# Expert feed-forward: wider weight slices in fewer slots, picks with the table as the stationary operand, prompt rows moved as 128 pieces

## What is computed

```python
aff = softmax(xf @ w_router)                  # (t, 16)
cap = 2 * t // 16                             # 16 of 128 rows, 128 of 1024 rows
gate, idx = top_k(aff.T, cap)
xe = xf[idx]                                  # (16, cap, 1024)
h = silu(xe @ w_e1) * (xe @ w_e3)             # three matrices of 1024x1024 per expert
ye = (h @ w_e2) * gate[..., None]
out = zeros_like(xf).at[idx].add(ye)
```

## Time and profile before

| | |
|---|---|
| median of 3 executions | 4532.65 us (4531.85 to 4542.73) |
| the profiled execution: first to last instruction | 4535.4 us; the page gives no other time for it |
| PE busy, share of the span | 3940.0 us, 87% |
| DVE / ACT / POOL busy | 2176.8 (48%) / 970.4 (21%) / 1048.6 (23%) us |
| DMA moved | 836.27 MB, mean 184 GB/s |
| mean granted TensorE clock | 0.924 |
| `experts`, first layer / second layer | about 1352 to 2260 us / 3580 to 4491 us |

### The profile page before, as it was taken

The page is one execution under the profiler, slowest core; times in us unless marked ns, Lnnn a source line. Parts: engine busy times, 40 slices in busy tenths (PEclk is TensorE's granted clock), DMA queues, the critical chain, the costliest instruction groups (busy, mean ns, idle before and its releaser), DMA issues. The chain is left out here.

```text
span 4535.4 us, 81543 instructions
## 1 busy us (share of the span) xinstructions
PE 3940.0 (87%) x34010; PEld 3088.9 (68%) x34010; DVE 2176.8 (48%) x4932; ACT 970.4 (21%) x1898; POOL 1048.6 (23%) x1092
## 2 busy tenths in 40 slices
PE   4999967888777999999779997788869599999994
PEld 3444546676347999999744444566654399999994
DVE  3335046566555445444453341566646544454444
ACT  2233134444110000000033322443431100000001
POOL 0036034453210000011040440445512001000003
PEclk9999978888888999999989998888879799999997
DMA  7556353331528999999664653243233299999995
GB/s 266 173 192 229 127 125 77 77 71 36 192 72 243 276 276 270 280 278 269 183 233 150 241 192 89 71 95 78 66 110 129 105 278 270 274 278 276 271 279 179
DMA packets 822587, 836.27 MB, mean 184 GB/s; under 512 B 92008, under 2 KB 667560, under 8 KB 816076
## 3 DMA queue, kind: packets, MB, share of 16 engines
q1 hardware_dynamic: 740172, 711.10, 52.5%
q10 hardware_dynamic: 70432, 81.03, 5.3%
q0 software_dynamic: 11616, 38.94, 3.8%
HBM read 698.83 MB, written 132.10 MB: 183 GB/s over the span
## 5 line engine op out<-in xcount | busy, mean ns | idle before, releaser
L2525 PE MATMUL ffn_hb<-ffn_xT,ffn_w 128*128 128x144 f32 x8192 | 1055.4, 288 | 11.2 <-DVE ffn_xT L2638 6.5
L2525 PEld LDWEIGHTS ffn_hb<-ffn_xT,ffn_w 128*128 128x128 f32 x8192 | 1025.8, 191 | 14.1 <-DVE ffn_xT L2638 6.7
L521 PE MATMUL front_acc<-front_w,front_xmT 128*128 128x512 f32 (+2 forms) x2304 | 879.2, 541 | 17.7 <-DVE front_xmT L782 17.5
L521 PEld LDWEIGHTS front_acc<-front_w,front_xmT 128*128 128x128 f32 x2304 | 438.2, 192 | 444.7 <-issue 417.7
L2533 PE MATMUL ffn_acc<-ffn_hT,ffn_w 128*128 128x144 f32 x4096 | 550.2, 288 | 0.0
L2533 PEld LDWEIGHTS ffn_acc<-ffn_hT,ffn_w 128*128 128x128 f32 x4096 | 521.4, 191 | 0.8
L2573 ACT ACTIVATE ffn_en<-ffn_hb 128x144 f32<-128x144 f32 x256 | 74.6, 291 | 1483.0 <-PE ffn_hb L2525 1483.0
L2457 POOL DMA_INDIRECT ffn_xe<-scratch_xhat,ffn_g_idx x34 | 34.5, 1015 | 1376.2 <-DVEq L2627 1376.2
L2672 DVE TENSOR_TENSOR ffn_hT<-ffn_en,ffn_hb 128x144 f32<-128x144 f32 x256 | 77.7, 304 | 528.8 <-ACT ffn_en L2573 527.9
L2247 PE MATMUL mixer_acc<-mixer_wout,mixer_oT 128*128 128x512 f32 x576 | 256.6, 604 | 3.2 <-DMA mixer_wout<-in_w_out 1.7
L2596 DVE TENSOR_SCALAR_CACHE_REDUCE ffn_junk<-ffn_row,ffn_pair 128x128 f32<-128x128 f32 (+2 forms) x324 | 245.4, 757 | 6.3 <-DVE ffn_yp L2645 4.9
(11 more groups left out here) (324 smaller groups left out, 5206.0 us busy)
## 6 DMA issues: line engine op xcount, KB each, us to landing
ffn_w<-in_w_e SPq DMA_DIRECT2D x768, 512.0 KB, 6.4
x_res<-in_w_mod SPq DMA_DIRECT2D x40, 1024.0 KB, 5.6
x_res<-scratch_proj SPq DMA_DIRECT2D x36, 768.0 KB, 6.2
scratch_proj<-front_out ACTq DMA_DIRECT2D x90, 256.0 KB, 2.2
ffn_row<-scratch_affT SPq DMA_DIRECT2D x36, 576.0 KB, 6.3
front_w<-in_w_in ACTq DMA_DIRECT2D x8, 2048.0 KB, 12.3
scan_qk<-scratch_qkv SPq DMA_DIRECT2D x16, 1024.0 KB, 9.8
scratch_qkv<-x_res SPq DMA_DIRECT2D x18, 768.0 KB, 3.5
```

The lines of the kernel that those rows point to most:

```text
L521: mm = pe.matmul(acc[:, U % 2, 0:size], xmT[:, k, t * P:(t + 1) * P], w[:, n % 2, k, 0:size], start=k == 0, stop=k == KD - 1)
L2525: mm = pe.matmul(hb[:, b, i * CAP:(i + 1) * CAP], w[:, r, k, :], xT[:, s, k, :], start=k == 0, stop=k == KD - 1)
```

## The change

Weights come as four slices of 256 hidden columns (1 MB from each matrix) in three slots. The picks use the table `pair`, widened to 32 columns, as the stationary operand and `sel` as the moving one: sample tiles 1 to 8 go in turn to the four 32-partition strips of one PSUM block, so that two tiles add up in each strip; DVE copies the block to SBUF (`copy_picks`), PE transposes it (`turn_picks`), and DVE adds the four strips (`rank_picked`). The prompt's 16 rows of 1024 are gathered and scattered as 128 pieces of 128 columns, eight per row, so that one 128x128 transpose replaces the eight small ones, and `turn_y` is no longer split. The copies of `acc` write sample and prompt columns to two tiles. The diff, cut to its core:

```diff
-    RING = 4
-    PER = KF // RING
+    RING = 3
+    WIDTH = 2
+    PER = KF // WIDTH
...
-        w1, w3, w2 = (st.sb(x, [P, RING, KD, P]) for x in ("w1", "w3", "w2"))
-        xe, xp = st.sb("xe", [P, D]), st.sb("xp", [CAP_P, D])
+        w1, w3 = (st.sb(x, [P, RING, KD, WIDTH * P]) for x in ("w1", "w3"))
+        w2 = st.sb("w2", [P, RING, WIDTH, D])
+        xe, xp = st.sb("xe", [P, D]), st.sb("xp", [P, P])
...
-        yT = st.sb("yT", [P, KD, CAP])
+        yT, yTp = st.sb("yT", [P, KD, CAP_S]), st.sb("yTp", [P, KD, CAP_P])
-        pair = st.sb("pair", [P, TILES, 2])
+        pair = st.sb("pair", [P, TILES, 32])
+        found = st.sb("found", [P, 2 * P])
...
-                    for j in range(KF):
-                        r = j % RING
-                        sp.wait_ge(w_used[r], e * PER + j // RING + 1)
+                    for j in range(0, KF, WIDTH):
+                        r = slot_of(e, j)
+                        c = slice(j * P, (j + WIDTH) * P)
+                        sp.wait_ge(w_used[r], fills(e, j) + 1)
+                        sp.dma_start(w1[:, r], T["w_e1"][l, e, :, c].rearrange("(k p) n -> p k n", p=P)).then_inc(w_in[r], 16)
+                        sp.dma_start(w3[:, r], T["w_e3"][l, e, :, c].rearrange("(k p) n -> p k n", p=P)).then_inc(w_in[r], 16)
+                        sp.dma_start(w2[:, r], T["w_e2"][l, e, c, :].rearrange("(a p) n -> p a n", p=P)).then_inc(w_in[r], 16)
-                        if j == 1:
+                        if j == 0:
                             sp.wait_ge(ranked, e + 3)
...
-                    for src, n, k in ((ye, P, 0), (yp, CAP_P, 1)):
+                    for src, dst, k in ((ye, T["moe"], 0), (yp, pieces("moe"), 1)):
...
-                    for k in range(KD):
-                        mm = pe.transpose(trp[:, k * CAP_P:(k + 1) * CAP_P], xp[:, k * P:(k + 1) * P], B.ident[0:CAP_P, 0:CAP_P])
-                    mm.then_inc(turned, 1)
+                    pe.transpose(xpT, xp[:], B.ident).then_inc(turned, 1)
+                def turn_y(e):
+                    pe.wait_ge(yT_done, e * 2 + 3)
+                    for k in range(KD):
+                        pe.transpose(tr[:, k * P:(k + 1) * P], yT[:, k, :], B.ident)
+                    pe.transpose(ypT, yTp[:].rearrange("p k n -> p (k n)"), B.ident).then_inc(y_turned, 1)
+                def sum_picks(e):
                     pe.wait_ge(sel_done, e + 2)
                     for t in range(1, TILES):
-                        pe.matmul(slot_s, sel[:, t, :], pair[:, t, :], start=t == 1, stop=t == TILES - 1)
-                    pe.matmul(slot_p, sel[:, 0, 0:CAP_P], pair[:, 0, :], start=True, stop=True).then_inc(picked, 1)
+                        q = (t - 1) % 4
+                        pe.matmul(trp[32 * q:32 * q + 32, 2 * P:3 * P], pair[:, t, :], sel[:, t, :], start=t <= 4, stop=t > 4)
+                    pe.matmul(found_p, pair[:, 0, :], sel[:, 0, 0:CAP_P].unsqueeze(1).to_broadcast([P, KD, CAP_P]), start=True, stop=True).then_inc(summed, 1)
+                def turn_picks(e):
+                    pe.wait_ge(copied, e + 2)
+                    pe.transpose(slot_s, found[:, 0:P], B.ident)
+                    pe.transpose(slot_p, found[0:32, P:2 * P], B.ident[0:32, 0:32]).then_inc(picked, 1)
...
                     def up_products(j):
-                        pe.wait_ge(w_in[r], (e * PER + j // RING) * 48 + 49)
+                        if j % WIDTH == 0:
+                            pe.wait_ge(w_in[r], fills(e, j) * 48 + 49)
...
                     def down_products(j):
-                        mm.then_inc(w_used[r], 1)
+                        if j % WIDTH == WIDTH - 1:
+                            mm.then_inc(w_used[r], 1)
...
                     up_products(0)
                     if not first:
-                        turn_y(e - 1, 0)
+                        turn_y(e - 1)
                     up_products(1)
                     if first:
-                        pick(1)
+                        sum_picks(1)
                     down_products(0)
-                    if not first:
-                        turn_y(e - 1, 1)
+                    if first:
+                        turn_picks(1)
...
-                    pick(e + 2)
+                    sum_picks(e + 2)
                     down_products(KF - 1)
+                    turn_picks(e + 2)
...
+                        act.activation(yT[:, k, :], y[:, :, 0:CAP_S], ACT.Copy)
+                        ins = act.activation(yTp[:, k, :], y[:, :, CAP_S:], ACT.Copy)
...
+                def copy_picks(e):
+                    dve.wait_ge(summed, e + 2)
+                    dve.tensor_copy(found[:, 0:P], found_s).then_inc(own, step())
+                    dve.tensor_copy(found[0:32, P:2 * P], found_p).then_inc(own, step())
+                    dve.wait_ge(own, step.n)
+                    dve.sem_inc(copied, 1)
...
+                    dve.tensor_scalar(ye[:], tr[:], picks[:, e, 1:2], None, ALU.mult).then_inc(own, step())
+                    dve.tensor_scalar(yp[:], ypT, picks[:, e, 3:4], None, ALU.mult).then_inc(own, step())
...
+                    copy_picks(e + 2)
+                    dve.wait_ge(w_used[slot_of(e, KF - 1)], fills(e, KF - 1) + 2)
+                    k, y = by_piece(0)
+                    dve.tensor_copy(yT[:, k, :], y[:, :, 0:CAP_S]).then_inc(own, step())
+                    dve.tensor_copy(yTp[:, k, :], y[:, :, CAP_S:]).then_inc(own, step())
                     rank_picked(e + 2)
```

More of the change, by code:

```diff
@@ L2421, in experts, with by_piece, slot_of, fills @@
         part = lambda c: acc[:, c // PER_BANK, (c % PER_BANK) * CAP:(c % PER_BANK + 1) * CAP]
+        pieces = lambda name: T[name].rearrange("r (k c) -> (r k) c", c=P)
+        def by_piece(b):
+            n = min(PER_BANK, KD - b * PER_BANK)
+            return slice(b * PER_BANK, b * PER_BANK + n), acc[:, b, 0:n * CAP].rearrange("p (k c) -> p k c", c=CAP)
+        def slot_of(e, j):
+            return (e * PER + j // WIDTH) % RING
+        def fills(e, j):
+            return (e * PER + j // WIDTH) // RING
         def turns(eng, body):
@@ L2454, in gather @@
                 def gather():
[L2455 to L2457 removed]
+                    for dst, src, k in ((xe, T["xhat"], 0), (xp, pieces("xhat"), 1)):
+                        at = bass.IndirectOffsetOnAxis(ap=g_idx[:, k:k + 1].bitcast(U32), axis=0)
+                        pool.indirect_dma_start(dst[:], None, src, at).then_inc(gathered, 16)
                 def scatter(e):
@@ L2584, in _ @@
                 dve.memset(counts[:], 0.0).then_inc(own, step())
+                dve.memset(pair[:], 0.0).then_inc(own, step())
                 dve.tensor_tensor(later[:], B.masks[:, 1, :], B.ident, ALU.subtract).then_inc(own, step())
+                dve.wait_ge(own, step.n)
                 dve.tensor_copy(pair[:, :, 0], B.ids[:, 0:TILES]).then_inc(own, step())
@@ L2622, in index @@
                         dve.wait_ge(own, step.n)
-                    dve.tensor_copy(idx[:, 0:1], token[:, 0, bass.ds(e, 1)]).then_inc(own, step())
-                    dve.tensor_copy(idx[0:CAP_P, 1:2], token[0:CAP_P, 1, bass.ds(e, 1)]).then_inc(own, step())
+                    dve.tensor_copy(idx[:], picks[:, e, 0:4:2]).then_inc(own, step())
                     dve.wait_ge(own, step.n)
@@ L2681, in body @@
                                 index(s_idx, e - 1, None)
-                                output(e - 1, 0)
+                                output(e - 1)
                             dve.wait_ge(row_in, e * 16 + 49)
-                        if j == 1 and not first:
-                            output(e - 1, 1)
                         if j == 5:
@@ L2691, in body @@
                             rank_tile(t)
+                    copy_picks(e + 2)
[3 more added lines that the diff above has]
+                    dve.tensor_copy(yTp[:, k, :], y[:, :, CAP_S:]).then_inc(own, step())
                     rank_picked(e + 2)
-                    dve.wait_ge(w_used[RING - 1], e * PER + PER + 1)
-                    dve.tensor_copy(yT[:, 0:PER_BANK, :].rearrange("p k n -> p (k n)"), acc[:, 0, 0:PER_BANK * CAP]).then_inc(own, step())
                     dve.wait_ge(own, step.n)
```

84 lines of the change are left out of this document (35 added, 49 removed).

## The result

Four executions of the changed kernel took 4473.70 to 4477.68 us, median 4476.71; four of the kernel before, beside it, had a median of 4532.25. The ratio is 0.9878, with a 95% interval of 0.9866 to 0.9890. The forecast was 4473 in a range of 4455 to 4505, so time and sign came out as predicted. By the medians the gain is 55.5 us for the 59.8 forecast. The profiled execution after, the fastest of its four, took 4473.70 us and spans 4471.9; the span before was 4535.4.

A forecast was written before the change was run, and what follows sets the result against it. The prediction took TensorE to bound the expert stage. Net gains of 29.9 us per layer, 59.8 for two, brought the profiled 4535.4 us to 4475.6, or 4473 in terms of the median, in a range of 4455 to 4505.

The forecast's parts named there:

- TensorE bounds the stage, and what leaves its order is gained: Expert stage: PE is busy throughout at clock 1.00; each expert gains 2.09 us, for a period of 50.39 us.
- Turning x and y: Transposes in each expert: one 128x128 transpose replaces eight small ones; gain 0.48 us at `x`, 0.77 at `y`.
- The pick: Pick in each expert: four strips run at once, so it takes 1.06 us for 1.90, gain 0.84.
- The work put at nothing: `turn_picks`, `turn_y` and POOL's 128 pieces in mid stage: waits are covered by other work and cost nothing.
- Weights in mid stage: Weight loads in mid stage: 350 GB/s and no stall, with 286 GB/s as the bound if wider runs bring nothing.
- rival 2: Mid stage: DMA becomes the bound and PE waits for weights, up to 1 us per expert; 4475 to 4508; chance 0.07.
- Start of each layer: First expert: up 2 must wait for all of pair 1, costing 4.0 us per layer; first pick 0, 2 either way.
- End of each layer: Last `turn_y` and scatter: one undivided chain, DVE ends earlier, larger scatter gives back 0.3; gain 1.2 us per layer.
- The sum: Per layer: experts 1 to 15 gain 31.4, expert 0 1.3, end 1.2, start -4.0; net 29.9 us.
- 1: Rival on the pick: strips of 32 columns do not overlap, 1.3 us more per expert, 4520 us; chance 0.08.
- 3: Rival on the clock: it falls in each expert, costing 3.7 us in 31 experts, 4588 us; chance 0.06 with similar losses.
- 4: Rival on the weight loads: the wider slices are the gain; expected to lose some 8 us alone; no chance of its own.

The follow-up runs named there:

- the run with old picks: Changed kernel with the picks as before (two moving columns over 128 stationary ones, no transposes of picks): median 4491.32 us, ratio 0.9903.
- the run without cover: Changed kernel with `turn_picks` directly behind `sum_picks`, no down product between: median 4488.89 us, ratio 0.9916.
- the narrow run: Changed kernel with its slices set back to 128 columns in four slots of one: median 4467.41 us, ratio 0.9850.
- the run with one strip: Changed kernel with the sixteen pick passes written to one strip of 32 partitions instead of four: median 4513.63 us, ratio 0.9963.
- the two lighter kernels: Changed kernel with seven of eight `w3` products left out, all loads kept: 4298.58 us with 128-column slices in four slots, 4264.89 with 256-column slices in three.

## Why the prediction was right

*TensorE bounds the stage, and what leaves its order is gained.* Right: 2.02 us per expert (2.09 predicted), PE busy throughout, clock 1.00.

*Turning x and y.* `y`: 0.98 us, as predicted to the hundredth. `x`: 0.98 for the 1.08 predicted, gain 0.58 for 0.48; the 0.97 for the eight large transposes held the step to the small shape (0.87 without it), which the ninth, of their own shape, does not need.

*The pick.* The mechanism, four strips at once, was right, and the passes took 0.47 us for 0.44 predicted. The terms around them were mis-sized: entering costs 0.09 us, as put down, but the prompt's product takes 0.31 for 0.22, and the two transposes with their entry 0.48 (0.38 and 0.10) for 0.30. In all 0.47 + 0.09 + 0.31 + 0.48 = 1.35 us for 1.06, and the gain is 0.55 in place of 0.84; the run with old picks says 0.56. Most of the missing 0.29 is made good, by luck, by 0.10 at `x` and about 0.1 at seams that no step had counted: 0.55 + 0.58 + 0.77 + 0.1 = 2.0.

*The work put at nothing.* Right for `turn_picks` (0.63 us under 1.96, by the run without cover), for `turn_y` in mid stage and for POOL: none shows up as a wait in the windows.

*Weights in mid stage.* No wait, as predicted, but the reasoning failed in one step: "just enough and no more" at 275 / 0.96 = 286 GB/s. The old slices gave 315, and the narrow run, at just this bound, shows no wait in mid stage: the price that rival 2 hung on it had no ground. Nor was the 419 GB/s set against it a figure for the new slices: it belongs to runs of 4 KB and longer, and 1 KB runs gave 379 where they were waited for.

*Start of each layer.* The step that failed in size, hidden by an opposite error. From the row load to up 2 it was 1411.55 - 1401.96 = 9.59 us and is 15.12: 5.53 more; up 2 itself, at the lower clock, takes 6.48 for 5.86: 0.62 more, 6.15 in all for the 4.0 put down. The kernel with narrow slices, all else as changed, needs 1403.51 - 1393.80 = 9.71 us from the row load to up 2, so the slices make 5.41 of the 15.12; by the stage sums they cost 5.3 us per layer there and 6.0 alone. The 5.35 that the prediction had first, at 294 GB/s, was nearer than the 4.0 to which it came down for faster runs. The extra 1.57 MB at the 346 to 396 GB/s of the windows above would be 4.0 to 4.5 us by itself. That the rest is the gather of expert 1, which now falls wholly into the wait (issued at 1402.87 us; before at 1407.16, 4.4 us ahead of up 2), is argued, not shown. Against that, the stretch from the first pick to the row load shrank from 1401.96 - 1376.28 = 25.68 to 1396.49 - 1372.85 = 23.64: 2.04 us. Of these, 1.29 lie between the first pick and the turning of `x` (10.11 us before, 8.82 after), which "shorter products and added copies and transposes about cancel" had put at 0 with 2 to either side; the other 0.75, turning `x` of expert 0 at the low clock, had no term. From the first pick to the end of up 2 the sum is 41.13 before and 45.24 after, 4.1 more. The 4.0 was right as a sum by luck, and wrong in both its parts.

*End of each layer.* From ACT's first copy to the next stage's first load: 4491.35 - 4469.98 = 21.37 before, 4428.18 - 4408.24 = 19.94 after: 1.43 in the second layer for the 1.2 predicted, 2.00 in the first. POOL starts 4.78 us after ACT, where it was 6.80. The transposes start only 0.20 us later behind ACT's copy (1.09 for 0.89), not 0.6; the scatter and what follows it give back 0.59, not 0.3.

*The sum.* In the first layer it can be split without remainder, at the row loads, the turning of `x` in experts 0 and 15 and ACT's first copy of the last `acc`. Before (PE's and ACT's timelines):

```profile
2223.93 1.04 PE L2490 MATMUL ffn_tr<-masks_sb,ffn_xe 128*128 128x128 f32 x8
2241.52 0.83 ACT L2577 ACTIVATE ffn_yT<-ffn_acc 128x432 f32<-128x432 f32 x2 [5.64 <-PE ffn_acc L2533]
```

After:

```profile
2194.43 1.04 PE L2508 MATMUL ffn_tr<-masks_sb,ffn_xe 128*128 128x128 f32 x8
2210.30 0.49 ACT L2596 ACTIVATE ffn_yT<-ffn_acc 128x384 f32<-128x384 f32 x1 [4.60 <-PE ffn_acc L2553]
```

| stretch of the first layer | before | after | gain |
|---|---|---|---|
| row loads to turning `x` in expert 0 (1436.84, 1437.53) | 85.25 | 89.23 | -3.98 |
| fifteen experts, to turning `x` in expert 15 | 787.09 | 756.90 | 30.19 |
| to ACT's first copy (turning `x`, the pick's products) | 17.59 | 15.87 | 1.72 |
| to the next stage's first load | 23.68 | 21.68 | 2.00 |
| sum | 913.61 | 883.68 | 29.93 |

The prediction had -4.0, 31.4 for the fifteen experts, 1.3 and 1.2. That 29.93 meets its 29.9 so closely is luck: 1.2 too much in the experts stands against 0.4 and 0.8 too little behind them.

*The rivals.* 1: refuted as a description of the changed kernel, confirmed as a price by the run with one strip. 2: no wait in mid stage at either width. 3: the clock was 1.00 in mid stage, and in the first expert, where the old pick had the low clock behind it (down 0 took 3.90 us), down 0 behind the new pick takes 2.23; with the old picks in the changed kernel it took 3.40. 4: the slices alone are 11.9 us slower in the stages.

Open are what limits the two lighter kernels, and how the longer wait at the start divides exactly between the pair's bytes and the gather.

## What to carry to other kernels

Where one engine is busy for a whole stage, price each small instruction group by start-to-start differences and look for products that write different strips of PSUM: they ran four at once here, and the same sixteen products in one strip would have undone the gain. When a prefetch unit is made coarser, look at the first consumer of each stage and not at the average: the steady state did not notice, the start lost 5 to 6 us per layer, and moving one load in front of a wait (but behind the transfer that the engine needs first) gave 24 us, more than the new pick. Judge small edits by the stretch that they touch: the unchanged stretches moved by several us between kernels, and one median agreed with a theory that its own profile refutes. And a sum that meets the forecast does not vouch for its terms.

## What was not expected of the hardware

- The busy share of the DMA engines is no gauge of what is left: 275 GB/s at 0.96, 286 at 1.00 and 315 at 1.11 with the same 512-byte runs, and 286 at 0.87 with 1 KB runs.
- A load of 3.15 MB that has the DMA engines to itself runs at 82 GB/s from 0.4 to 1.4 us after its issue, at 253 in the next microsecond, and then at 346 to 410. Behind a row load it takes longer to get there: 88 and 239 GB/s, for 2 us each. In that run the last 1.1 us before PE went on carried 19 GB/s.
- Sixteen passes of 128 columns over 32 stationary ones take 0.47 us into four strips and 1.77 into one, at a clock of 1.00, with all 128 rows in use in both.
